# A two-layer diffusion trunk on one core: the shift's product as rows of the weight slab, the eviction moved behind six chunks, Q's rotary chunks in another order, and K's second copies by DMA

## The chip, the core and the metric

The kernel runs on one core of one Trainium2 chip. Times are device microseconds of one execution. The change is judged by the median of such times, beside runs of the kernel before. Five engines work side by side and meet only at semaphores: PE (TensorE, matrix products), ACT (ScalarE), DVE (VectorE), POOL (GpSimd) and SP, which here only issues DMAs.

## What is computed

Two layers over 768 tokens (256 of context, CTX, and 512 latent, LAT) of width 1024. Layer 0 mixes by gated linear attention, layer 1 by windowed attention with 16 query heads on 2 key heads. Each has a SwiGLU FFN of 2816 behind it. The part that matters here is how every projection gets its input, and what layer 1 does with Q and K:

```python
for i in range(DEPTH):
    hx = rmsnorm(x, norm_mix[i]) * (1.0 + sc1) + sh1        # sc, sh: scale and shift from silu(c) @ w_ada
    hc = rmsnorm(ctx, norm_mix[i]) * (1.0 + csc1) + csh1
    ox, oc = gla_mixer(hx, hc, ...) if i % 2 == 0 else swa_mixer(hx, hc, ..., cos, sin, not last)
    x = x + g1 * ox
    x = x + g2 * swiglu(rmsnorm(x, norm_ffn[i]) * (1.0 + sc2) + sh2, ffn_w_in[i], ffn_w_out[i])
    # the same for ctx, unless it is the last layer
# swa_mixer
q, k, v = jnp.split(h @ w_qkv + b_qkv, [SWA_Q, SWA_Q + SWA_KV], axis=-1)
qx = apply_rope(qx, cos, sin)
kx = apply_rope(kx, cos, sin)
# softmax over |i-j| <= 128, all context keys and a sink logit per head, then @ v and @ w_o
return rmsnorm(x, norm_final)
```

## The kernel before

**Slabs.** All weights come as slabs of 1024 rows by 256 columns (`w_raw`). Products are made in float32r: a slab is split into `w_hi` (ACT, function `split` of `act`, L1145) and `w_lo = w_raw - w_hi` (DVE, L1611), the input into a high and a low part as well, and PE makes three products, hi·hi, hi·lo and lo·hi. All of them have the line of the helper `mm`, L549. A slab has 8 chunks k of 128 rows. With both token segments a chunk is 12 matmuls (2 column blocks, 3 products, 256 and 512 columns), with LAT alone 6. Slab n lies in buffer n % 2. SP loads slab n+2 when PE has ended slab n.

**The slab without norm.** The first slab behind each residual sum starts before the norm is known: `first_slab` of `pe` multiplies `x * scale` (not normed), since `(x * rstd * scale + shift) @ w = rstd * ((x * scale) @ w) + shift @ w`. There are three: slab F0 (first slab of layer 0's FFN, both segments), KV0 (K and V of layer 1, both segments) and F1 (first slab of layer 1's FFN, LAT alone). In between its chunks PE also sums the squares (`statistics`, at k = 3) and spreads 1/rms over the partitions (`spread`, at k = 4, with LAT alone at k = 5), and ACT copies that into `rb` (`spread_out`, L1179). At the end PE makes `shift @ w`: for each of 2 column blocks and 8 chunks three matmuls with the weights as stationary operand and 2 moving columns (shift for LAT and for CTX, `sh_hi` and `sh_lo`), 48 in all.

**What DVE and ACT do meanwhile.** They make h, the normed input of the next slab, chunk by chunk: DVE `scaled` (L1666), ACT `h_hi` (L1190, `modulate`), DVE `h_lo` (L1675, `normal`). PE waits for each chunk of h in slab n+1. DVE's and ACT's queues are written out in order. After four chunks DVE waits for the end of slab n, copies `shift @ w` (`bz`, L1989 or L2089) and evicts the slab times `rb`; then chunks 4 to 7 follow. In the FFN ACT puts Silu on it. In slabs F0 and F0+1 PE also makes a piece of `silu(c) @ w_ada` (`unit`: 8 products with 32 stationary columns in four column groups of the array), which ACT copies to a row (`u_row`), PE turns with the 2-column matrix `sel`, and DVE adds to `mods`.

**K and Q of layer 1.** DVE evicts K into `y_rot`, ACT adds the bias, SP swaps the rotary halves by 4 DMAs of 32 partitions (`swap_halves`, L475), DVE makes cos and sin (L2068, L2072, L2077). ACT and DVE then write K's high and low part into `k_st`, each twice: heads 0 and 1, each into partitions 0 to 63 and 64 to 127 (L1488, L2108, 4 instructions each). Q has four slabs Q0 to Q0+3 and eight chunks f of 128 rows. For each, ACT `raw_q` (L1504) evicts and adds the bias, SP swaps, DVE turns (`turn_q`), ACT makes the high part (`high`, L1511) and DVE the low part (`low`, L2118). Slabs Q0+1 to Q0+3 are loaded into `ada_w`, one after the other: SP issues the next when DVE has ended `w_lo` of the one before. Behind it all come 64 rounds of attention: PE `scores`, DVE `maxima` (L2170), ACT exp (L1571), and so on, two rounds of scores ahead.

```python
        def raw_q(f):                       # act; may overwrite q_rot of f-3 only when low(f-3) is done
            if f < 7:
                act.wait_ge(ql_ok, max(2 * f - 3, 1))
```

Of the kernel before, what the change touches and what calls it, by code (L numbers as in the profile page):

```python
# [24 lines left out]
F32 = mybir.dt.float32  # L25
# [42 lines left out]
def trunk(nc, x, c, ctx_in, c_ctx, w_ada, b_ada, norm_mix, norm_ffn, gla_w_in, gla_w_gate_up, gla_b_gate_up,  # L68
# [159 lines left out]
    zg_ok, zp_ok, zk_ok = sems("zg_ok", "zp_ok", "zk_ok")  # L228
    amul_ok, t_ok, hh_ok, h_ok = sem("amul_ok"), sem("t_ok"), sem("hh_ok"), sem("h_ok")
# [16 lines left out]
    wp_ok = sem("wp_ok")  # L246
# [92 lines left out]
    def _(sp):  # L339
# [207 lines left out]
    def _(pe):  # L547
# [182 lines left out]
        def first_slab(n, e, segs, turn=None):  # L730
# [8 lines left out]
            for k in range(DC):  # L739
# [355 lines left out]

        pe.wait_ge(sink_ok, 9)
# [43 lines left out]
    def _(act):  # L1140
# [253 lines left out]
        def ffn(l, n0, segs):  # L1394
# [211 lines left out]
    def _(dve):  # L1606
# [369 lines left out]
        def ffn(l, m, n0, segs):  # L1976
# [3 lines left out]
            def first(n, sh):  # L1980
# [16 lines left out]
                normal(2 * l + 1, 2 * l, segs, sh, 4, 8)  # L1997
# [100 lines left out]
        normal(2, KV_EDGE, (LAT,), 48, 4, 8)  # L2098
# [170 lines left out]
```

## Time and profile before

| | us |
|---|---|
| median of 3 runs | 1707.42 |
| lowest and highest | 1706.73, 1715.22 |
| the profiled execution | 1717.53 |
| its span, first to last instruction | 1715.8 |
| PE busy | 1669.9 (97%) |
| DVE busy | 716.6 (42%) |
| ACT busy | 592.1 (35%) |
| TensorE's mean granted clock | 0.978 |

Busy time is the time in which an engine had an instruction under way. A busy PE can still be slow: the granted clock is 1.00 at 2.4 GHz and 0.50 at 1.2 GHz, and the page of the profile shows it per slice of the span. The rows further down are from four views: the timeline (instructions in order of time, merged where alike, with the idle time before one and what ended it), windows (busy time, granted clock and DMA share of a stretch), the DMA view, and the page itself.

### The profile page before, as it was taken

The page shows a single profiled execution, that of the slowest core. Times are in us where ns is not written, and L with a number is a line of the kernel's source. Part 1 is how long each engine was busy: PE and PEld are TensorE (multiplying, and loading weights), DVE is VectorE, ACT ScalarE, POOL GpSimd, SP SyncE. Part 2 cuts the span into 40 slices and gives each one's busy share as a digit, 9 for nine tenths or more (in the row PEclk, how much of TensorE's full clock was granted, in tenths as well). Part 3 has the DMA queues.
Part 4 walks back from the last instruction along what each step waited for, and adds up shares of the span by engine and source line. Part 5 has one row for each costly group of instructions (what it writes and reads, how often), then busy time and mean ns, then how long its engine had stood idle before and what let it go on. Part 6 is the DMA issues. An engine that isn't in the chain of part 4 may idle for free.

```text
span 1715.8 us, 24363 instructions
## 1 busy us (share of the span) xinstructions
PE 1669.9 (97%) x9948; PEld 1395.5 (81%) x9948; DVE 716.6 (42%) x1044; ACT 592.1 (35%) x890; POOL 103.4 (6%) x95
## 2 busy tenths in 40 slices
PE   7999999999999999999999999979999999999998
PEld 5889988888888888888888889756768888888886
DVE  5414536444532222222222245777764533333334
ACT  5224457443422211222111233457653422222223
POOL 0000000000000000000000000035550000000003
PEclk8999999999899999999999999979999899999999
DMA  9332200014243343343343322320002233333332
GB/s 337 88 123 92 81 25 26 25 58 139 74 124 98 108 137 98 113 132 98 119 127 98 92 68 74 86 68 2 2 1 74 74 98 98 98 98 98 89 90 91
DMA packets 197022, 155.30 MB, mean 91 GB/s; under 512 B 6658, under 2 KB 194222, under 8 KB 196942
## 3 DMA queue, kind: packets, MB, share of 16 engines
q1 hardware_dynamic: 196942, 154.18, 29.9%
q8 instruction: 57, 0.93, 0.2%
q14 instruction: 23, 0.19, 0.0%
HBM read 149.71 MB, written 2.10 MB: 88 GB/s over the span
## 4 chain that ended last, share of the span: by engine, by line
PE 89%; ACT 3%; DVE 3%; DMA 2%; SPq 1%; issue 1%; DVEq 0%; ACTq 0%
PE ps L549 87%; PE ps L1073 2%; DMA ada_pre<-in_w_ada 1%; ACT w_hi L1145 1%; DVE w_lo L1611 1%; DMA q_sw<-q_rot 0%; SPq L356 0%; DMA w_raw<-in_ffn_w_in 0%; DVE q_st L2118 0%; SPq L475 0%; PE ps L846 0%; DVE k_st L2108 0%; DVE r_act L1906 0%; ACT tmp L1285 0%; ACT k_st L1488 0%
## 5 line engine op out<-in xcount | busy, mean ns | idle before, releaser
L549 PE MATMUL ps<-h_hi,w_hi 128*128 128x256 f32 (+1 forms) x1392 | 422.2, 362 | 2.0 <-DVE w_lo L1611 1.5
L549 PE MATMUL ps<-h_lo,w_hi 128*128 128x256 f32 (+1 forms) x1392 | 411.1, 354 | 0.0
L549 PE MATMUL ps<-h_hi,w_lo 128*128 128x256 f32 (+1 forms) x1392 | 410.9, 354 | 0.0
L1611 DVE TENSOR_TENSOR w_lo<-w_raw,w_hi 128x2048 fp32r<-128x2048 f32 (+1 forms) x88 | 197.4, 2244 | 375.9 <-ACT w_hi L1145 375.8
L1145 ACT ACTIVATE w_hi<-w_raw 128x2048 fp32r<-128x2048 f32 (+1 forms) x88 | 165.1, 1876 | 408.9 <-DMA w_raw<-in_ffn_w_in 244.2
L549 PEld LDWEIGHTS ps<-h_hi,w_hi 128*128 128x128 f32 x1392 | 256.9, 190 | 49.6 <-issue 15.6
L549 PEld LDWEIGHTS ps<-h_lo,w_hi 128*128 128x128 f32 x1392 | 264.1, 190 | 36.9
L549 PEld LDWEIGHTS ps<-h_hi,w_lo 128*128 128x128 f32 x1392 | 263.9, 190 | 37.1
L549 PE MATMUL ps<-a_hi,w_hi 128*128 128x512 f32 (+1 forms) x528 | 159.7, 357 | 0.0
L549 PE MATMUL ps<-a_lo,w_hi 128*128 128x512 f32 (+1 forms) x528 | 157.9, 353 | 0.0
L549 PE MATMUL ps<-a_hi,w_lo 128*128 128x512 f32 (+1 forms) x528 | 157.8, 353 | 0.0
L537 POOL TENSOR_SCALAR pr<-pr,rden 128x384 f32<-128x384 f32 x64 | 84.1, 1314 | 896.2 <-DVE rden L2203 896.1
L549 PEld LDWEIGHTS ps<-a_hi,w_hi 128*128 128x128 f32 x528 | 98.0, 188 | 17.5 <-issue 4.1
L549 PEld LDWEIGHTS ps<-a_hi,w_lo 128*128 128x128 f32 x528 | 99.2, 188 | 14.2
L549 PEld LDWEIGHTS ps<-a_lo,w_hi 128*128 128x128 f32 x528 | 99.2, 188 | 14.0
L1426 ACT ACTIVATE tmp<-ps 128x512 f32<-128x512 f32 (+1 forms) x63 | 30.8, 524 | 199.4 <-PE ps L549 199.4
L1693 DVE SCALAR_TENSOR_TENSOR xT<-ps,mods,xT 128x256 f32<-128x256 f32 (+3 forms) x96 | 57.7, 657 | 98.5 <-PE ps L549 98.5
L2019 DVE TENSOR_TENSOR tmp<-tmp,ps 128x512 f32<-128x512 f32 (+1 forms) x63 | 35.8, 596 | 138.2 <-ACT tmp L1426 138.2
L549 PEld LDWEIGHTS ps<-k_st,q_st 128*128 128x128 f32 x320 | 44.2, 198 | 32.8 <-issue 21.1
L549 PE MATMUL ps<-k_st,q_st 128*128 128x256 f32 x320 | 55.3, 305 | 10.5 <-ACT pr L1571 10.5
L2170 DVE TENSOR_REDUCE row_max<-ps 128x1 f32<-128x513 f32 (+1 forms) x64 | 48.4, 756 | 27.6 <-PE ps L549 27.4
L1159 ACT ACTIVATE sq<-xT 128x768 f32<-128x768 f32 (+1 forms) x32 | 23.7, 740 | 101.0 <-DVE xT L1693 100.8
(242 smaller groups left out, 2043.4 us busy)
## 6 DMA issues: line engine op xcount, KB each, us to landing
w_raw<-in_ffn_w_in SPq DMA_DIRECT2D x88, 512.0 KB, 5.2
ada_w<-in_w_ada SPq DMA_DIRECT2D x41, 1024.0 KB, 5.4
w_raw<-in_ffn_w_out SPq DMA_DIRECT2D x32, 512.0 KB, 5.6
w_raw<-in_gla_w_in SPq DMA_DIRECT2D x24, 512.0 KB, 5.0
ada_pre<-in_w_ada SPq DMA_DIRECT2D x7, 1024.0 KB, 11.3
w_raw<-in_ffn_w_out SPq DMA_DIRECT2D x16, 384.0 KB, 3.7
w_raw<-in_gla_w_o SPq DMA_DIRECT2D x8, 512.0 KB, 7.1
w_raw<-in_swa_w_o SPq DMA_DIRECT2D x8, 512.0 KB, 4.6
```

What stands on the lines that cost most here:

```text
L537: pool.tensor_scalar(pr[i % 3][:, 0:384], pr[i % 3][:, 0:384], rden[:, i % 4:i % 4 + 1], None, ALU.mult)\
L549: return pe.matmul(o, w, r, start=start, stop=stop, skip_group_check=skip)
L1073: last = pe.transpose(bank(bk, (t - a) * P, P), pr[i % 3][:, t * P:(t + 1) * P], ident[:, :])
L1145: act.activation(w_hi[s][:, 0:kc, :], raw_of(n)[:, 0:kc, :], ACT.Copy).then_inc(whi_ok, 1)
L1159: act.activation(sq[ch % 2][:, a:T], xT[:, ch, a:T], ACT.Square).then_inc(sq_ok, 1)
L1426: last = act.activation(tmp[s][:, sg[0]:sg[1]], seg(3 * s, 0, sg), ACT.Silu)
L1611: dve.tensor_tensor(w_lo[s][:, 0:kc, :], raw_of(n)[:, 0:kc, :], w_hi[s][:, 0:kc, :].bitcast(F32), ALU.subtract).then_inc(wlo_ok, 1)
L1693: last = dve.scalar_tensor_tensor(xs, seg(3 * s, ch, sg), mods[:, bass.ds(gate + d0 + ch, 1), int(sg == CTX)], xs, ALU.mult, ALU.add)
L2019: last = dve.tensor_tensor(tmp[2 + s][:, sg[0]:sg[1]], tmp[s][:, sg[0]:sg[1]], seg(3 * s, 1, sg), ALU.mult)
L2170: dve.tensor_reduce(row_max[:, i % 4:i % 4 + 1], ps[:, b0 * 512:b0 * 512 + nk + 1], AX.X, ALU.max)\
```

## The change

There are four parts.

1. `shift @ w` is made with the shift as stationary operand: `sh_c` holds per chunk 32 columns, two of them the shifts and the rest zero, and the moving operand is the weight chunk of 256 columns in plain float32, `w_hi` and then `w_lo`. The 16 products go to four column groups of the array, 32 PSUM partitions each. They stand ahead of chunk k = 6 in the slab. ACT copies the result to `b_row` (`bias_row`), and at the slab's end PE turns it with `sel`, two products of 2 columns, which also sum the four groups.
2. In the three stages ACT copies `rb` before it splits the next slab. DVE makes chunk 0 of h before it splits, and the eviction stands behind six chunks of h in F0 and F1 (before: four), behind all eight in KV0.
3. `raw_q(7)` stands behind `high(6)`; `high` and `low` of f = 2 stand behind `turn_q(3)` on DVE; `low(6)` moves behind the first reciprocal of the attention rounds.
4. ACT and DVE write each half of K once. The other copy of each head is a DMA from `k_st` to `k_st`, 64 partitions each, issued by SP behind the swap of f = 1 and ahead of the load of slab Q0+3. PE waits for both ahead of the first scores.

```diff
@@ tiles
-    sh_hi = at("sh_hi", TM + 10 * ROW, [P, DC, 2], F32R)
-    sh_lo = at("sh_lo", TM + 10 * ROW + 64, [P, DC, 2], F32R)
+    sh_c = at("sh_c", TM + 10 * ROW, [P, DC, 32])
+    b_row = at("b_row", TM + 4 * ROW, [P, 256])
@@ sync
             swap_halves(f + 2, q_rot[sw_set(f)], q_sw[sw_set(f)], sw_in[sw_set(f)])
+            if f == 1:
+                sp.wait_ge(ql_ok, 1)
+                for g in range(2):
+                    sp.dma_start(k_st[64 - 64 * g:128 - 64 * g, :, g, :].bitcast(F32),
+                                 k_st[64 * g:64 * g + 64, :, g, :].bitcast(F32))\
+                      .then_inc(in_k, 16)
@@ tensor, first_slab
+                if k == 6:
+                    pe.wait_ge(rbs_ok, e + 1)
+                    pe.wait_ge(sh_ok, 2 * e + 2)
+                    for j, w in enumerate((w_hi, w_lo)):
+                        for c_ in range(DC):
+                            g = 32 * (c_ % 4)
+                            last = mm(bank(7, 0, 256)[g:g + 32, :], sh_c[:, c_, :], w[s][:, c_, :].bitcast(F32),
+                                      j == 0 and c_ < 4, j == 1 and c_ >= 4)
+                    last.then_inc(bw_done, 1)
...
-            pe.wait_ge(rbs_ok, e + 1)
-            pe.wait_ge(sh_ok, 2 * e + 2)
+            pe.wait_ge(br_ok, e + 1)
             for ch in range(2):
-                blk = slice(ch * P, (ch + 1) * P)
-                for k in range(DC):
-                    for j, (w, r) in enumerate(((w_hi, sh_hi), (w_hi, sh_lo), (w_lo, sh_hi))):
-                        last = mm(bank(7, 2 * ch, 2), w[s][:, k, blk], r[:, k, :], k == 0 and j == 0,
-                                  k == DC - 1 and j == 2, skip=True)
+                last = mm(bank(7, 2 * ch, 2), b_row[:, ch * P:(ch + 1) * P], sel[:, :], True, True)
             last.then_inc(slab_done, 1)
@@ scalar
+        def bias_row(e):
+            act.wait_ge(bw_done, e + 1)
+            act.activation(b_row[:, :], bank(7, 0, 256), ACT.Copy).then_inc(br_ok, 1)
@@ scalar, F0 and F1
+                spread_out(5 + 2 * l, a)
                 split(n + 1)
-                spread_out(5 + 2 * l, a)
-                modulate(2 * l + 1, 2 * l, segs, sh, 0, 4)
+                modulate(2 * l + 1, 2 * l, segs, sh, 0, 2)
+                bias_row(2 * l)
+                modulate(2 * l + 1, 2 * l, segs, sh, 2, 6)
...
-                modulate(2 * l + 1, 2 * l, segs, sh, 4, 6)
+                modulate(2 * l + 1, 2 * l, segs, sh, 6, 8)
                 split(n + 2)
-                modulate(2 * l + 1, 2 * l, segs, sh, 6, 8)
@@ scalar, KV0 and Q
+        spread_out(6, 0)
         split(Q0)
-        spread_out(6, 0)
-        modulate(2, KV_EDGE, (LAT,), 48, 0, 4)
+        modulate(2, KV_EDGE, (LAT,), 48, 0, 2)
+        bias_row(KV_EDGE)
+        modulate(2, KV_EDGE, (LAT,), 48, 2, 8)
...
-        modulate(2, KV_EDGE, (LAT,), 48, 4, 6)
         split(Q0 + 1)
-        modulate(2, KV_EDGE, (LAT,), 48, 6, 8)
         act.wait_ge(yr_ok, 1)
         for g in range(2):
-            for r in range(2):
-                last = act.activation(k_st[64 * r:64 * r + 64, 0, g, :], y_rot[64 * g:64 * g + 64, :], ACT.Copy)
+            last = act.activation(k_st[64 * g:64 * g + 64, 0, g, :], y_rot[64 * g:64 * g + 64, :], ACT.Copy)
...
-        for f in range(4, DC):
-            raw_q(f)
-            high(f - 1)
+        raw_q(4)
+        high(3)
+        raw_q(5)
+        high(4)
+        raw_q(6)
+        high(5)
+        high(6)
+        raw_q(7)
@@ vector, F0 and F1 (KV0: 0 to 1, split, 1 to 8, then the eviction)
+                normal(2 * l + 1, 2 * l, segs, sh, 0, 1)
                 split(n + 1)
-                normal(2 * l + 1, 2 * l, segs, sh, 0, 4)
+                normal(2 * l + 1, 2 * l, segs, sh, 1, 6)
                 dve.wait_ge(slab_done, n + 1)
...
-                normal(2 * l + 1, 2 * l, segs, sh, 4, 8)
+                normal(2 * l + 1, 2 * l, segs, sh, 6, 8)
                 split(n + 2)
@@ vector, K's low part: two instructions of four; Q and the first attention round
+        turn_q(3)
         low(2)
-        turn_q(3)
...
         turn_q(6)
-        low(6)
...
+            if i == 0:
+                low(6)
```

Three places show what stands in the queues. First PE, at the end of slab F0 (`w_hi_56` and `w_lo_60` are its weights, `w_hi_57` those of slab F0+1); chunk 5's last products, before and after:

```order
L549 MATMUL ps<-h_hi,w_lo_60 128x512
L549 MATMUL ps<-sh_hi,w_hi_56 128x2
L549 MATMUL ps<-sh_lo,w_hi_56 128x2
L549 MATMUL ps<-sh_hi,w_lo_60 128x2
...
L549 MATMUL ps<-ada_w,c_pre 32x256 x8
L549 MATMUL ps<-h_hi,w_hi_57 128x256
```

```order
L557 MATMUL ps<-h_lo,w_hi_56 128x512
L557 MATMUL ps<-h_hi,w_lo_60 128x256
L557 MATMUL ps<-h_hi,w_lo_60 128x512
L557 MATMUL ps<-w_hi_56,sh_c 32x256 x8
L557 MATMUL ps<-w_lo_60,sh_c 32x256 x8
L557 MATMUL ps<-h_hi,w_hi_56 128x256
L557 MATMUL ps<-h_hi,w_hi_56 128x512
```

Of before this is the slab's end (the three kinds with `sh` stand there 16 times each); of after it is the border of chunks 5 and 6, with two chunks of the slab still behind it.

Second DVE in stage F1, from 1/rms on (`w_lo_60` belongs to slab F1+1, `tmp` is the evicted slab):

```order
L1631 RECIPROCAL rstd<-std 128x4
L1611 TENSOR_TENSOR w_lo_60<-w_raw_58,w_hi_56 128x2048
L1666 SCALAR_TENSOR_TENSOR scaled_126<-xT,amul,rb 128x512
L1666 SCALAR_TENSOR_TENSOR scaled_127<-xT,amul,rb 128x512
L1675 SCALAR_TENSOR_TENSOR h_lo<-scaled_126,mods,h_hi 128x512
```

```order
L1655 RECIPROCAL rstd<-std 128x4
L1689 SCALAR_TENSOR_TENSOR scaled_126<-xT,amul,rb 128x512
L1698 SCALAR_TENSOR_TENSOR h_lo<-scaled_126,mods,h_hi 128x512
L1635 TENSOR_TENSOR w_lo_60<-w_raw_58,w_hi_56 128x2048
L1689 SCALAR_TENSOR_TENSOR scaled_127<-xT,amul,rb 128x512
L1689 SCALAR_TENSOR_TENSOR scaled_126<-xT,amul,rb 128x512
L1698 SCALAR_TENSOR_TENSOR h_lo<-scaled_127,mods,h_hi 128x512
```

The scaling of chunk 1 moved from ahead of the first `h_lo` to behind `w_lo`. It is what ACT's chunk 1 of h waits for, and `bias_row` stands behind that.

Third DVE in Q, from the turning of f = 2 (`q_rot_110`) on:

```order
L2077 TENSOR_TENSOR q_rot_110<-q_rot_110,q_sw_114 128x512
L1611 TENSOR_TENSOR w_lo_60<-ada_w,w_hi_56 128x2048
L2118 TENSOR_TENSOR q_st<-q_rot_110,q_st 64x512 x2
L2068 TENSOR_TENSOR q_rot_108<-q_rot_108,cosT 128x512
L2072 TENSOR_TENSOR q_sw_112<-q_sw_112,sinT 128x512
L2077 TENSOR_TENSOR q_rot_108<-q_rot_108,q_sw_112 128x512
L2118 TENSOR_TENSOR q_st<-q_rot_108,q_st 64x512 x2
```

```order
L2101 TENSOR_TENSOR q_rot_110<-q_rot_110,q_sw_114 128x512
L1635 TENSOR_TENSOR w_lo_60<-ada_w,w_hi_56 128x2048
L2092 TENSOR_TENSOR q_rot_108<-q_rot_108,cosT 128x512
L2096 TENSOR_TENSOR q_sw_112<-q_sw_112,sinT 128x512
L2101 TENSOR_TENSOR q_rot_108<-q_rot_108,q_sw_112 128x512
L2141 TENSOR_TENSOR q_st<-q_rot_110,q_st 64x512 x2
L2141 TENSOR_TENSOR q_st<-q_rot_108,q_st 64x512 x2
```

The low part of f = 2 now stands behind the turning of f = 3; the other pairs of turning and low part stay as they were, except that of f = 6.

## Rows read from the trace of the kernel before

**Rows 1.** Timeline of PE, stage F0: start, us, instruction, count.
```profile
457.72 0.51 PE L549 MATMUL ps<-h_hi,w_lo 128*128 128x256 f32 x2
458.07 0.16 PE L549 MATMUL ps<-sh_hi,w_hi 128*128 128x2 f32 x1
...
465.39 1.93 PE L549 MATMUL ps<-ada_w,c_pre 128*32 128x256 f32 x16
...
481.93 0.50 PE L549 MATMUL ps<-sel,u_row 128*128 128x2 f32 x4
...
486.70 1.07 PE L549 MATMUL ps<-ada_w,c_pre 128*32 128x256 f32 x16
487.70 0.62 PE L549 MATMUL ps<-h_hi,w_hi 128*128 128x256 f32 x2
```

**Rows 2.** Windows of F0: us, busy PE, PEld, DVE, ACT, POOL, PEclk, DMA, GB/s.
```profile
455.00:461.00 6.00, 6.00 (x47) 5.63 (x45) 5.29 (x10) 2.96 (x5) 0.00 (x0) 1.00 0.01 3
461.00:471.00 10.00, 10.00 (x51) 8.23 (x51) 4.29 (x10) 3.92 (x7) 0.00 (x0) 0.51 0.23 70
```

**Rows 3.** Timeline of DVE, stage F0.
```profile
449.17 2.29 DVE L1611 TENSOR_TENSOR w_lo<-w_raw,w_hi 128x2048 fp32r<-128x2048 f32 x1 [2.28 <-ACT w_hi L1145]
...
455.05 0.48 DVE L1666 SCALAR_TENSOR_TENSOR scaled<-xT,amul,rb 128x256 f32<-128x256 f32 x1
...
457.25 0.48 DVE L1666 SCALAR_TENSOR_TENSOR scaled<-xT,amul,rb 128x256 f32<-128x256 f32 x1
...
466.51 1.01 DVE L1994 TENSOR_TENSOR tmp<-ps,rb 128x256 f32<-128x256 f32 x2
```

**Rows 4.** Timeline of ACT, stage F0.
```profile
449.93 0.81 ACT L1179 ACTIVATE rb<-ps 128x768 f32<-128x768 f32 x1 [0.79 <-PE ps L549]
...
477.01 1.92 ACT L1145 ACTIVATE w_hi<-w_raw 128x2048 fp32r<-128x2048 f32 x1 [4.26 <-DMA w_raw<-in_ffn_w_in]
```

**Rows 5.** Timeline of stage F1, all engines.
```profile
1339.07 0.60 ACT L1179 ACTIVATE rb<-ps 128x512 f32<-128x512 f32 x1 [0.89 <-PE ps L549]
...
1340.26 0.39 PE L549 MATMUL ps<-rs_hi,w_hi 128*128 128x512 f32 x1
...
1342.74 0.75 DVE L1666 SCALAR_TENSOR_TENSOR scaled<-xT,amul,rb 128x512 f32<-128x512 f32 x1
...
1344.19 0.75 DVE L1666 SCALAR_TENSOR_TENSOR scaled<-xT,amul,rb 128x512 f32<-128x512 f32 x1
...
1364.11 0.39 PE L549 MATMUL ps<-h_hi,w_hi 128*128 128x512 f32 x1
```

**Rows 6.** Timeline of K, Q and the first attention round, all engines.
```profile
1076.11 1.12 ACT L1475 ACTIVATE y_rot<-y_rot,bz 128x256 f32<-128x256 f32 x2 [11.38 <-DVE y_rot L2093]
...
1083.40 2.29 DVE L1611 TENSOR_TENSOR w_lo<-ada_w,w_hi 128x2048 fp32r<-128x2048 f32 x1
...
1087.65 3.42 ACT L1488 ACTIVATE k_st<-y_rot 64x768 fp32r<-64x768 f32 x4 [4.95 <-DVE y_rot L2077]
...
1091.10 3.85 DVE L2108 TENSOR_TENSOR k_st<-y_rot,k_st 64x768 fp32r<-64x768 f32 x4 [3.48 <-ACT k_st L1488]
...
1107.85 0.69 DVE L2068 TENSOR_TENSOR q_rot<-q_rot,cosT 128x512 f32<-128x512 f32 x1 [0.68 <-DMA q_sw<-q_rot]
...
1129.88 1.40 DVE L2118 TENSOR_TENSOR q_st<-q_rot,q_st 64x512 fp32r<-64x512 f32 x2 [0.69 <-ACT q_st L1511]
...
1132.15 1.28 ACT L1571 ACT_TABLE_LOAD   x1 [1.65 <-DVE neg_max L2173]
...
1134.28 1.23 PE L549 MATMUL ps<-k_st,q_st 128*128 128x256 f32 x4 [9.48 <-ACT pr L1571]
```

**Rows 7.** DMA view, issues of 1060 to 1140: count, KB each, us to landing.
```profile
q_sw<-q_rot SPq DMA_DIRECT2D x32, 64.0 KB, 2.0
```

**Rows 8.** Windows in Q: slab load and swaps; swaps alone.
```profile
1104.00:1105.00 1.00, 1.00 (x6) 0.81 (x5) 0.97 (x2) 0.64 (x2) 0.00 (x0) 1.00 1.10 389
1113.00:1114.00 1.00, 1.00 (x6) 0.84 (x5) 0.97 (x2) 0.00 (x0) 0.00 (x0) 1.00 0.51 125
```

More of the change, by code:

```diff
@@ L155, in trunk @@
     rb = at("rb", TM + 9 * ROW, [P, T])
-    sh_hi = at("sh_hi", TM + 10 * ROW, [P, DC, 2], F32R)
-    sh_lo = at("sh_lo", TM + 10 * ROW + 64, [P, DC, 2], F32R)
-    bz = at("bz", TM + 10 * ROW + 128, [P, 2, 2])
+    sh_c = at("sh_c", TM + 10 * ROW, [P, DC, 32])
+    bz = at("bz", TM + 10 * ROW + 2048, [P, 2, 2])
+    b_row = at("b_row", TM + 4 * ROW, [P, 256])
     rs_hi = at("rs_hi", A, [P, DC, LX], F32R)
@@ L228, in trunk @@
     zg_ok, zp_ok, zk_ok = sems("zg_ok", "zp_ok", "zk_ok")
+    bw_done, br_ok, bt_done = sems("bw_done", "br_ok", "bt_done")
     amul_ok, t_ok, hh_ok, h_ok = sem("amul_ok"), sem("t_ok"), sem("hh_ok"), sem("h_ok")
@@ L244, in trunk @@
     osq_ok, f1_ok, f2_ok, goh_ok, go_ok = sems("osq_ok", "f1_ok", "f2_ok", "goh_ok", "go_ok")
-    wp_ok = sem("wp_ok")
+    wp_ok, in_k = sem("wp_ok"), sem("in_k")
     sw_in = sems("sw_in0", "sw_in1", "sw_in2", "sw_in3")
@@ L1093, in weighted @@
                 last.then_inc(pv_done, 1)
+        pe.wait_ge(in_k, 32)
         pe.wait_ge(sink_ok, 9)
@@ L1648, in shifts @@
         def shifts(e, sh):
-            dve.tensor_copy(sh_hi[:, :, :], mods[:, sh:sh + 8, :]).then_inc(sh_ok, 1)
+            dve.memset(sh_c[:, :, :], 0.0).then_inc(sh_ok, 1)
             dve.wait_ge(sh_ok, 2 * e + 1)
-            dve.tensor_tensor(sh_lo[:, :, :], mods[:, sh:sh + 8, :], sh_hi[:, :, :].bitcast(F32), ALU.subtract)\
-               .then_inc(sh_ok, 1)
+            dve.tensor_copy(sh_c[:, :, 0:2], mods[:, sh:sh + 8, :]).then_inc(sh_ok, 1)
         def normal(l, e, segs, sh, c0, c1):
@@ L2085, in _ @@
         inverse(6)
+        normal(2, KV_EDGE, (LAT,), 48, 0, 1)
         split(Q0)
-        normal(2, KV_EDGE, (LAT,), 48, 0, 4)
+        normal(2, KV_EDGE, (LAT,), 48, 1, 8)
         dve.wait_ge(slab_done, KV0 + 1)
@@ L2097, in _ @@
         dve.sem_inc(out_free[KV0 % 2], 1)
-        normal(2, KV_EDGE, (LAT,), 48, 4, 8)
         split(Q0 + 1)
@@ L2106, in _ @@
         for g in range(2):
-            for r in range(2):
-                last = dve.tensor_tensor(k_st[64 * r:64 * r + 64, 1, g, :], y_rot[64 * g:64 * g + 64, :],
-                                         k_st[64 * g:64 * g + 64, 0, g, :].bitcast(F32), ALU.subtract)
+            last = dve.tensor_tensor(k_st[64 * g:64 * g + 64, 1, g, :], y_rot[64 * g:64 * g + 64, :],
+                                     k_st[64 * g:64 * g + 64, 0, g, :].bitcast(F32), ALU.subtract)
         last.then_inc(ql_ok, 1)
```

## The prediction, made before the changed kernel ran

> **What bounds the kernel now.** I read the page first: PE is busy for nearly the whole span, so time can only come out of PE's own work, out of its clock, or out of the few stretches where it waits. Then the timeline of PE around the three slabs without norm, with the granted clock of the same stretches, and last DVE, ACT and SP there, since they say whether PE can use an earlier start.
>
> In stage F0 the 48 products of two columns run from 458.07 to the unit at 465.39: 7.3 us [rows 1]. The clock was 1.00 until 461 and 0.51 on the mean from 461 to 471, while PE worked without a gap [rows 2]: the products' first 3 us ran at 2.4 GHz, then all went at 1.2 GHz for 10 us. So the unit took 1.93 us where its like takes 1.07 at 486.70 [rows 1], and half of 5.6 us of ordinary work is lost behind the products. KV0 and F1 look alike.
>
> Between KV0 and attention PE does not set the pace: it stood for 9.48 us before 1134.28, until ACT had made the first exp. ACT's table load at 1132.15 waited for DVE's first maximum, and DVE came to it only with the last low part of Q, at 1129.88 [rows 6]. There the chain of DVE, ACT and SP is what counts, from K's first row at 1076.11 on.
>
> The sum is made against the profiled execution, 1717.53 us. The median of the runs is 10.1 us lower; I take the gain over to it unchanged, as all its terms lie on the chain that ends last in both.
>
> **Stage F0.** PE: slab F0's own products end at 458.07. A unit of 8 products costs 1.00 us from start to start at full clock (486.70 to 487.70), 16 cost 2.0, now inside the slab. So the slab ends at 460.1. The turning with sel is what stands at 481.93: 0.50 us, about 0.36 net, 460.5 [rows 1]. The unit follows, 461.5. ACT's b_row must be there at 460.1: rb is done at 450.74 [rows 4]; ACT splits until 452.6, makes chunk 0 until 453.7; DVE's h_lo until 454.45, its w_lo (2.25) until 456.7 [rows 3], scaled(1) until 457.8; ACT's chunk 1 until 458.5, b_row until 458.9. 1.2 us to spare.
>
> Slab F0+1 needs 8 chunks of 12 matmuls, pairs of them 0.347 us apart (457.72 to 458.07) [rows 1]: 16.7 plus a turning, from 461.5 to 478.5, if h keeps up. DVE makes a chunk in 2.20 us (455.05 to 457.25) [rows 3]: chunk 1 at 459.3, chunk 5 at 468.0, needed at 471.9. The eviction (1.9, as at 466.51 [rows 3]) and the table load for Silu (1.28, as at 1132.15 [rows 6]) push chunk 6 to 473.9 and chunk 7 to 476.1; PE comes to them at 474.4 and 476.4. It just fits. Late next is DVE: ACT splits slab F0+2 only behind chunk 7, 475.3 to 477.2, though its weights should have come by 471 (the wait for them ended at 477.01 [rows 4], and all goes 5.8 us earlier). DVE's w_lo ends at 479.5, the store to mods behind it at 479.7, and PE's next unit waits for that store: 1.2 us. Unit, then slab F0+2 at 480.75 instead of 487.70 [rows 1]: **7.0 us**. Bounds: 8.2 without that wait; 2 if the wait lowers the clock (up to half of 10 us, rows 2).
>
> **Stage F1.** There is no unit and a chunk is only 6 matmuls, 1.37 us. Chunk 6 starts at 1340.26 [rows 5]; plus 2.0 and two chunks the slab's products end at 1345.0. But b_row is late. rb is there at 1339.67 [rows 5]; ACT's split 1.9, chunk 0 0.7, DVE's h_lo 0.7, w_lo 2.25, scaled(1) 0.7, ACT's chunk 1 0.7, b_row 0.35: 1347.0. PE stands for 2.0 us, ends the slab at 1347.4 (before: 1351.0), and takes slab F1+1. DVE needs 1.45 us for a chunk (1342.74 to 1344.19) [rows 5]; chunk 5 is ready at 1352.5, then come the eviction and the Silu, chunk 6 at 1356.6, where PE wants it at 1355.6. Behind chunk 7 come ACT's split, until 1358.4, and w_lo, until 1360.65. Slab F1+2 starts at 1360.7 instead of 1364.11 [rows 5]: **3.4 us**, not the 7.6 that the removed products promise. Bounds: 2 (each of the 13 steps 0.1 later), 5 (PE alone).
>
> **KV0 to the first exp.** PE's slab ends 5 to 6 us earlier, as in F0, but DVE is not there. Before, ACT had done four chunks of h when its wait of 11.38 us began, at 1064.7 [rows 6], DVE at 1065.5. Now w_lo (2.25) and ACT's split (1.9) stand behind rb and no longer in the wait for it: 1069.7 for four chunks, and with four more at 1.45, less 0.5 at the end, 1075.0. Eviction and bias come behind them, so y_rot starts where it did, at 1076.2 (1076.11 [rows 6]), and the swap lands as before. What was queued between goes: ACT's split is done at 1080.1, DVE's w_lo starts at 1080.15 instead of 1083.40, 3.25 us. PE waits 1.6 us for it ahead of slab Q0+1; that is hidden. K's high part is 1.71 instead of 3.42, its low part 1.93 instead of 3.85 [rows 6]: 3.6 us. So raw_q(0) starts 6.9 us earlier, and so does w_lo of Q0+2.
>
> Then SP. The two copies of K carry 2 x 393 KB ahead of slab Q0+3 and the swap of f = 2, which DVE awaited at 1107.85 already [rows 6]. Swaps move 125 GB/s at a DMA share of 0.51 [rows 8], so 245 at full share: the copies take 3.2 us of it. Their two issues take 1.2 and lie before the slab's; with that the swap lands 2.3 us later against the rest: at about 1103.4, not 1107.85 minus 6.9. From here 4.45 us are left. Behind it the order saves: low(6), 1.40 us [rows 6], goes into the gap while PE makes the third scores, and turn_q(3) ahead of low(2) hides a wait for ACT of 0.7; with the waits for swaps as they now fall I get the table load at 1125.0 instead of 1132.15: **7.2 us**. Bounds: 10 if the copies cost nothing; 5 if they take twice their share. Raw_q(7) and its swap come late, at 1129.4; DVE wants it at 1129.5. PE's slab Q0+3 waits 3 us for w_lo; hidden, its end at 1118.7 is far ahead of the first maximum at 1123.
>
> The memset of sh_c and the copy take about 0.2 us more than the two casts they replace and end ahead of 1/rms; nothing.
>
> Sum: 7.0 + 7.2 + 3.4 = 17.6. 1717.5 - 17.6 = 1699.9; on the median 1707.4 - 17.6 = **1689.8 us**.
>
> The Trainium skill, "TensorEngine Tiling (Array Packing)", Key Properties, says that changing the tiling mode drains the array, and the block now stands inside a slab, with two changes more. By the trace the pair behind a unit takes 0.62 us (487.70) where 0.51 is usual (457.72) [rows 1]: 0.1 a change, so 0.6 us at most over three stages, which would make it 1690.4.
>
> The Trainium skill, "DMA: Bandwidth & Descriptors", Where 436 GB/s comes from, has SBUF to SBUF bound only by the fabric, at 435 GB/s. K's copies would be 1.8 us by it, an estimate, not 3.2. The rows show 125 GB/s in pieces of 2 KB; by the page the sum would be about 1.4 us better.
>
> **Rivals.**
> *The copies are cheap.* For it: a slab load moves 389 GB/s in rows 8, and K's pieces are 3 KB long. At that rate they take 2.0 us and the swap lands 1.2 earlier; at nothing 2.9. Time 1687 to 1689, taken as 1687.5. The page's rule on the fabric points here.
> *The new waits lower the clock.* PE now stands 1.2 us behind F0+1, 2.0 and 1.0 in F1. Against: they are short, the one before 1134.28 was 9.48 [rows 6]. For: nothing in the rows excludes it, and a stretch at half speed like that of rows 2 costs up to 5 us. In F0 it is fully exposed, in F1 partly: 5 to 8 us less gain, 1696.
> *The half speed was not the two-column products' alone.* The sums of squares, the spreading, the new block with 32 of 128 columns stationary, and sel now lie within 17 us. If the clock still falls, each of F0 and F1 gives back up to 5 us: 1699.8. Against: the clock was 1.00 from 455 to 461, behind the slab's statistics and spreading [rows 2], and the unit at 486.70 ran at full speed [rows 1].
> *Slower: the copies block SP's queue.* One swap DMA of 64 KB lands 2.0 us after issue [rows 7]. If a copy's time goes with its bytes at that pace, 393 KB take 12.3 us each, 24.6 together, 21.8 more than in my sum. Slab Q0+3, the swap of f = 2 and with them the whole chain of Q come later, and PE's first scores wait: 17.6 - 21.8 = -4.2, 1711.6. It decides from about 20 us for both copies. Against: several swap DMAs overlap, 0.6 us apart, at 125 GB/s, so 2.0 us is mostly latency.
>
> **How the numbers follow.** Forecast 0.62, copies cheap 0.13, waits lower the clock 0.13, half speed stays 0.08, slower 0.04. The forecast's own bounds are 1685 to 1695; with the cases beside it I take 1683 to 1700. What a measurement can tell from no change is 0.5%, 8.5 us. The forecast, the cheap copies and most of the third case gain more, 0.88; half speed stays and the rest of the third case are within, 0.08; slower 0.04.
>
> **What would show it.** PE's block of 32 matmuls of 256 columns takes 2.0 us, with the clock at 1.00 through all of F0 up to 480. b_row ends ahead of the slab in F0 and KV0, and PE waits about 2 us for it in F1. DVE's w_lo sets the start of slabs F0+2 and F1+2. The DMA k_st<-k_st takes 3 to 4 us and the wait for q_sw of f = 2 grows to about 3 us. The first exp is 13 to 15 us earlier, F0's gain counted in. I am wrong if the clock falls around 460, if PE waits for h in F0+1 by more than 1 us, or if the first exp comes late by a swap.

## The result and the profile after

| | before | changed |
|---|---|---|
| median, 12 runs each | 1712.82 us | 1700.05 us |
| lowest, highest | 1706.01, 1718.25 | 1696.43, 1701.98 |
| the profiled execution | 1717.53 | 1699.94 |
| its span | 1715.8 | 1698.2 |

The ratio is 0.9926, 95% interval 0.9907 to 0.9945: 12.8 us faster. I had 1689.8, range 1683 to 1700. Between the two profiled executions the gain is 17.6 us, as forecast; between the medians it is 4.8 us less, and before's median is 5.4 us above the one of three runs that I had started from (they are the first three of these twelve). Those two make the miss of 10.2 us. The 4.8 lies with before: its profiled execution was 4.7 us above its median, that of the changed kernel 0.1 below (1699.94 against 1700.05).

**F0.** Timeline of PE after, in the columns of [rows 1]:

```profile
453.33 1.07 PE L557 MATMUL ps<-w_hi,sh_c 128*32 128x256 f32 x16
454.21 1.05 PE L557 MATMUL ps<-w_lo,sh_c 128*32 128x256 f32 x16
...
459.53 0.50 PE L557 MATMUL ps<-sel,b_row 128*128 128x2 f32 x4
459.96 1.07 PE L557 MATMUL ps<-ada_w,c_pre 128*32 128x256 f32 x16
...
478.71 1.07 PE L557 MATMUL ps<-ada_w,c_pre 128*32 128x256 f32 x16 [0.39 <-DVE mods L1706]
```

PE's products with the shift (`sh_c`) now stand inside the slab; behind its last product come the turning (`sel`) and the unit, which takes 1.07 where it took 1.93. The wait for DVE's store to `mods` has come, 0.39 us in place of the 1.2 that I gave it. Windows of F0, KV0 and F1 after, in the columns of [rows 2]:

```profile
455.00:475.00 20.00, 20.00 (x134) 17.09 (x127) 17.99 (x34) 11.82 (x20) 0.00 (x0) 1.00 0.37 106
1062.00:1082.00 20.00, 18.38 (x85) 15.04 (x84) 13.88 (x19) 9.60 (x14) 0.00 (x0) 1.00 0.24 66
1334.00:1358.00 24.00, 21.95 (x96) 17.49 (x96) 15.76 (x20) 10.88 (x12) 0.00 (x0) 1.00 0.31 88
```

The granted clock is 1.00 in each: all three stages run at 2.4 GHz.

**K and Q.** Timeline of ACT, DVE and PE after, answering [rows 6]:

```profile
1068.25 1.12 ACT L1497 ACTIVATE y_rot<-y_rot,bz 128x256 f32<-128x256 f32 x2 [1.88 <-DVE y_rot L2118]
1072.23 2.29 DVE L1635 TENSOR_TENSOR w_lo<-ada_w,w_hi 128x2048 fp32r<-128x2048 f32 x1 [3.15 <-ACT w_hi L1159]
1076.49 1.70 ACT L1507 ACTIVATE k_st<-y_rot 64x768 fp32r<-64x768 f32 x2 [4.29 <-DVE y_rot L2101]
1078.22 1.92 DVE L2131 TENSOR_TENSOR k_st<-y_rot,k_st 64x768 fp32r<-64x768 f32 x2 [1.77 <-ACT k_st L1507]
...
1097.31 0.69 DVE L2092 TENSOR_TENSOR q_rot<-q_rot,cosT 128x512 f32<-128x512 f32 x1 [4.95 <-DMA q_sw<-q_rot]
...
1118.91 1.28 ACT L1595 ACT_TABLE_LOAD   x1
...
1121.04 0.93 PE L557 MATMUL ps<-k_st,q_st 128*128 128x256 f32 x4 [3.89 <-ACT pr L1595]
```

K's halves cost half. But DVE waited 4.95 us for the swap of f = 2, where it had waited 0.68. PE in turn waited 4.75 us for `w_lo` of slab Q0+3, where I had 3, and from there on ran at half speed:

```profile
1101.63 0.76 PE L557 MATMUL ps<-h_hi,w_hi 128*128 128x512 f32 x1 [4.75 <-DVE w_lo L1635]
```

The granted clock was 0.50 from 1101 to 1107. It cost nothing here, but by little: PE's first scores started at 1115.49, and DVE came to the first maximum at 1116.78, straight from turning f = 6.

**F1.** Timeline after, all engines, answering [rows 5]:

```profile
1325.30 0.60 ACT L1193 ACTIVATE rb<-ps 128x512 f32<-128x512 f32 x1 [3.51 <-PE ps L557]
1325.79 1.91 ACT L1159 ACTIVATE w_hi<-w_raw 128x2048 fp32r<-128x2048 f32 x1
...
1329.01 2.28 DVE L1635 TENSOR_TENSOR w_lo<-w_raw,w_hi 128x2048 fp32r<-128x2048 f32 x1
...
1332.62 0.36 ACT L1198 ACTIVATE b_row<-ps 128x256 f32<-128x256 f32 x1
...
1333.03 0.61 PE L557 MATMUL ps<-sel,b_row 128*128 128x2 f32 x4 [1.56 <-ACT b_row L1198]
...
1342.94 0.50 PE L557 MATMUL ps<-h_hi,w_hi 128*128 128x512 f32 x1 [1.01 <-DVE h_lo L1698]
1346.98 0.49 PE L557 MATMUL ps<-h_hi,w_hi 128*128 128x512 f32 x1 [1.03 <-DVE w_lo L1635]
```

PE waits three times, for `b_row`, for chunk 6 and for `w_lo`. New too are ACT's 3.51 us of idling ahead of `rb`: its split now stands behind.

### The profile page after: what moved, and what is told of

The parts are those of the page before. It is cut to its first block, busy times and chain, and to the rows that moved or that the text cites. A ratio compares the mean times of both kernels' runs of the same rounds, so it can differ in the third digit from the quotient of the medians.

```text
span 1698.2 us, 24292 instructions
## 1 busy us (share of the span) xinstructions
PE 1649.9 (97%) x9912; PEld 1372.2 (81%) x9912; DVE 715.0 (42%) x1042; ACT 591.1 (35%) x891; POOL 104.0 (6%) x95
## 4 chain that ended last, share of the span: by engine, by line
PE 86%; ACT 5%; DVE 5%; DMA 1%; SPq 1%; issue 1%; DVEq 0%; ACTq 0%
PE ps L557 84%; PE ps L1086 2%; ACT w_hi L1159 1%; DVE w_lo L1635 1%; DVE h_lo L1698 1%; DVE scaled L1689 1%; DMA ada_pre<-in_w_ada 1%; SPq L357 1%; ACT h_hi L1209 0%; DMA q_sw<-q_rot 0%; DMA w_raw<-in_ffn_w_in 0%; SPq L476 0%; PE ps L859 0%; DVE r_act L1929 0%; ACT tmp L1304 0%
## 5 line engine op out<-in xcount | busy, mean ns | idle before, releaser
L2043 DVE TENSOR_TENSOR tmp<-tmp,ps 128x512 f32<-128x512 f32 (+1 forms) x63 | 35.8, 596 | 140.1 <-ACT tmp L1446 140.1
```

The lines of the kernel that those rows point to most:

```text
L2043: last = dve.tensor_tensor(tmp[2 + s][:, sg[0]:sg[1]], tmp[s][:, sg[0]:sg[1]], seg(3 * s, 1, sg), ALU.mult)
```

## Where the time went, stage by stage

Each row is one profiled execution. F0: rb of F0 to rb of KV0. Q: rb of KV0 to ACT's table load ahead of the first exp. F1: std of F1 to the third `a_lo` behind it, that of the first slab inside the loop. The last column is the us at half speed behind the shift's products in F0, KV0 and F1. All rows but "before" and "changed" are experiments, told below.

| kernel | execution | F0 | Q | F1 | at half speed |
|---|---|---|---|---|---|
| before | 1717.5 | 608.5 | 73.7 | 42.2 | 10.2, 10.2, 10.2 |
| before_3 | 1711.3 | 606.8 | 71.1 | 42.2 | 6.8, 6.8, 10.2 |
| before_4 | 1705.4 | 604.9 | 71.5 | 40.6 | 3.4, 6.8, 6.8 |
| q_only | 1709.5 | 605.9 | 71.5 | 42.2 | 3.4, 6.8, 10.2 |
| changed | 1699.9 | 601.2 | 68.4 | 38.95 | 0, 0, 0 |
| after_again | 1700.1 | 601.3 | 68.5 | 38.95 | 0, 0, 0 |
| block_only | 1697.7 | 601.0 | 66.75 | 35.9 | 0, 0, 0 |
| k_engines | 1700.4 | 601.2 | 67.45 | 38.9 | 0, 0, 3.4 |
| k_late | 1691.8 | 601.2 | 64.0 | 38.95 | 0, 0, 0 |
| old_ffn | 1694.5 | 601.3 | 68.0 | 35.9 | 0, 0, 0 |
| split_first | 1694.4 | 600.6 | 67.9 | 35.7 | 0, 0, 0 |
| combo | 1688.2 | 601.4 | 61.2 | 35.85 | 0, 0, 0 |
| best | 1685.2 | 600.8 | 61.5 | 35.8 | 0, 0, 0 |

From profile to profile F0 gave 7.3 us (forecast 7.0), Q 5.3 (7.2), F1 3.2 to the loop (3.4). The three make 15.8. The remaining 1.8 came from outside them: 0.7 ahead of rb of F0, 0.5 between the table load and F1, 0.6 behind F1. My sum had nothing there, and it is scatter as far as I can tell: the second profile of the changed kernel lies 0.8 above, 1.8 below and 1.1 above the first in these. That the profiles came out at 17.6 was partly luck.

## The experiments

**The spread of before.** No edit; the kernel before against itself, then two single profiles.

> The kernel before, unchanged, against itself. So far its executions lie at two levels, 1706 to 1708 and 1714 to 1718 us; the profiled one was at 1717.5 with a mean clock of 0.978, while the changed kernel's lie between 1696.4 and 1702.0. Theory A (the levels are the clock's): the time of an execution falls with its mean granted clock, 1 us for each 0.001 or so, the executions at 1707 show about 0.985, those at 1716 about 0.978, and a profile at the lower level shows one or two of the stretches at half speed shorter or gone that the profile at 1717.5 has (362 to 369, 1127 to 1141, 1147 to 1154). Rival B: the clock is the same at both levels, and they differ by a wait, for instance a DMA that lands late. If A holds, the gain of 17.6 us between two profiles isn't the gain between medians, since before was profiled at its upper level.

Measured: median 1711.36 against 1710.48, ratio 1.0008 (0.999 to 1.0026), 1705.85 to 1718.01. Theory A holds as to the clock: over 64 executions of before on four chips (these 12 and those run beside this and the later experiments), from 1704.2 to 1719.0 us, the mean clock runs from 0.987 down to 0.977, and 0.001 of it goes with 1.4 us, where A had about 1 (correlation -0.97). What I had taken for two levels is a spread. This profile fell on 1717.98, again at the top, so where the half speed goes it could not tell.

> The kernel before, unchanged, one profile more. Its two profiles so far fell on its longest executions (1717.5 and 1718.0, 77 us at half speed), while its executions reach down to 1704. With Q's parts alone changed a profile at 1709.5 showed the stretch behind F0's products of two columns 3.4 us long instead of 10.2, the one in KV0 6.8 instead of 10.2. Theory A: the length of these stretches changes from execution to execution by 3.4 us at a time; a profile below 1710 us shows F0, KV0 or F1 with less than 10.2 us each, and rb of F0 to rb of KV0 takes 605.9 where F0 has 3.4 us at half speed and 608.4 where it has 10.2. Rival B: the three stretches are always 10.2 us long in this kernel and the others, at the start, at 362 and in attention, make the spread.

> The same once more, with the same expectations: under A a profile below 1710 us has a shorter stretch at half speed in F0, KV0 or F1; under B all three are 10.2 us long again and the start, 362 to 369 and attention make the difference.

Measured: 1711.32 and 1705.35. Windows over the same three stages, of before, before_3 and before_4 in turn:

```profile
455.00:475.00 20.00, 20.00 (x117) 17.30 (x116) 12.78 (x25) 7.87 (x13) 0.00 (x0) 0.74 0.34 99
1062.00:1082.00 20.00, 20.00 (x99) 18.01 (x98) 9.72 (x17) 7.26 (x11) 0.00 (x0) 0.74 0.06 14
1334.00:1358.00 24.00, 24.00 (x119) 21.23 (x118) 15.18 (x23) 10.78 (x13) 0.00 (x0) 0.79 0.23 62
```

```profile
455.00:475.00 20.00, 20.00 (x125) 17.34 (x125) 13.73 (x27) 8.11 (x13) 0.00 (x0) 0.83 0.31 95
1062.00:1082.00 20.00, 20.00 (x105) 17.52 (x105) 11.74 (x18) 7.54 (x11) 0.00 (x0) 0.83 0.05 13
1334.00:1358.00 24.00, 24.00 (x111) 20.80 (x110) 16.20 (x23) 9.89 (x13) 0.00 (x0) 0.79 0.16 44
```

```profile
455.00:475.00 20.00, 20.00 (x133) 17.17 (x133) 11.68 (x24) 9.70 (x15) 0.00 (x0) 0.91 0.36 106
1062.00:1082.00 20.00, 20.00 (x92) 17.00 (x92) 11.95 (x17) 9.83 (x13) 0.00 (x0) 0.83 0.23 66
1334.00:1358.00 24.00, 24.00 (x110) 20.37 (x110) 13.72 (x19) 9.07 (x12) 0.00 (x0) 0.86 0.32 88
```

PE is busy throughout, and still the clock column of F0 reads 0.74, 0.83 or 0.91: (1 - 0.74) x 20 x 2 is 10.4 us at half speed, 0.83 gives 6.8, 0.91 gives 3.6. Theory A holds, B does not: the same products cost another amount in each execution. Only before_4 fell below 1710 us as A had asked; its F0 took 604.9 us where A had 605.9 for 3.4 us at half speed, and that one microsecond I did not follow. Against before_4 the changed kernel gains 3.7, 3.1 and 1.6 us in the three stages, 8.4; against the profile that I had, 7.3, 5.3 and 3.2, 15.8. In F0 the gain is 7.3, 5.6 and 3.7 where before had 10.2, 6.8 and 3.4 us at half speed; by that step some 2 us would be left without any (an estimate). The Trainium skill, "TensorE: Matmul & The Clock Gate", What's actually happening, says that the monitor's window runs free and does not restart with the kernel, so that a change of clock depends on where the work falls in it. The three profiles are in keeping with it, with 3.4, 6.8 and 10.2 us behind the same instructions in F0; that it is the reason no run here shows.

**The block alone.** Before with the shift's product as in the changed kernel, nothing else:

```diff
+                if k == 6:
+                    pe.wait_ge(rbs_ok, e + 1)
...
-                modulate(2 * l + 1, 2 * l, segs, sh, 0, 4)
+                modulate(2 * l + 1, 2 * l, segs, sh, 0, 2)
+                bias_row(2 * l)
+                modulate(2 * l + 1, 2 * l, segs, sh, 2, 4)
```

> The kernel before with the shift's product as 32 products of 256 columns inside the slab alone; the eviction stays behind four chunks of h, Q's order and K's copies as before. Theory A (the block is nearly all of the change): F0 gains 7 us, F1 2 to 4, and at KV0 the eviction starts 5.5 us earlier since DVE had waited for PE's slab there (four chunks were ready at 1065.5, the slab at 1074.9), and the whole chain of Q moves with it: 14.5 to 16.5 us off a profile at 1717.5, a median of 1698 to 1702. Rival B (as my sum had it, KV0's and Q's 7.2 us come out of the new order of ACT and DVE, the turning one ahead and K's copies): F0 and F1 gain 10.4 and KV0 to the first exp 1 to 2, a median near 1704. On the levels: if the 48 products of two columns make them, this kernel's executions lie within 6 us of each other as the changed kernel's; if not, two levels 10 us apart stay.

Measured: 1697.05 (1691.54 to 1697.77), ratio 0.9911 (0.9886 to 0.9936). Theory A, and beyond its numbers: its profile lies 19.8 us below 1717.5, where A had 14.5 to 16.5, and F1 gained 6.3, where A had 2 to 4. The block is all of the change, and F1 is 3 us shorter than in the changed kernel. The intervals of the two ratios overlap; the stage times set the two kernels apart. The granted clock was 1.00 in the windows of all three stages here as well. Timeline of ACT and DVE in its F1:

```profile
1322.62 1.92 ACT L1151 ACTIVATE w_hi<-w_raw 128x2048 fp32r<-128x2048 f32 x1 [0.74 <-DMA w_raw<-in_ffn_w_in]
1324.56 2.29 DVE L1626 TENSOR_TENSOR w_lo<-w_raw,w_hi 128x2048 fp32r<-128x2048 f32 x1 [2.48 <-ACT w_hi L1151]
1325.38 0.60 ACT L1185 ACTIVATE rb<-ps 128x512 f32<-128x512 f32 x1 [0.85 <-PE ps L550]
...
1328.84 0.36 ACT L1190 ACTIVATE b_row<-ps 128x256 f32<-128x256 f32 x1
```

Here split and w_lo lie in the time in which ACT and DVE wait for PE's spreading, and b_row is 3.9 us earlier, long before the slab ends. Its executions spread over 6.2 us, where I had 6 at most and before has 14.

**Q's parts alone.** Before, with K's copies by DMA and Q's order as in the changed kernel.

> The kernel before with Q's new order and K's second copies by DMA at their place in the changed kernel, the shift's product left as it was. Theory A: K's halves 3.6 and the order 2.1, less 4.3 of wait for the swap of f = 2, leave 1.4 us from rb of KV0 to the first exp, 73.3 against 74.7; median within 0.15% of before's. Rival B (the order and the copies bring what my sum had beside w_lo, 4 us): 70.7. On the levels: the executions spread over 10 to 14 us as before's do, since the stretches of two columns are still there, and the time goes with the clock; if its profile falls at a low level, it shows which stretches at half speed are missing there.

Measured: 1710.29 against 1709.32, ratio 1.0002 (0.9985 to 1.002). The median moved by less than 0.15% and the executions spread over 12.4 us, as A had it, and B's 4 us are out. From y_rot to the table load it took 55.1 us, against 56.0 in the profile of before, 55.5 in before_3 and 55.9 in before_4: 0.4 to 0.9 us, less than A's 1.4. The whole stage, 71.5 us, is no shorter than that of before_3 and before_4 (71.1 and 71.5), which had the same 6.8 us at half speed in KV0. The copies' wait takes back most of what K's halves save, as in the changed kernel.

**Where K's copies stand.** k_late is the changed kernel with one line other:

```diff
-            if f == 1:
+            if f == 3:
                 sp.wait_ge(ql_ok, 1)
```

k_engines has no DMA; both copies are ACT's and DVE's, four instructions each, as before.

> The changed kernel with K's two copies issued behind the swap of f = 3, no longer ahead of slab Q0+3's load and the swap of f = 2. DVE waited 4.95 us for that swap at 1097.31, where before it waited 0.68. Theory A (the copies' traffic and SP's queue delay the slab and the swap): that wait falls to about 0.7, ACT's wait for slab Q0+3 (4.54) to under 1, the first exp comes 3.5 to 4.5 us earlier, and the time falls to about 1696, in no case does PE wait for the copies ahead of the first scores. Rival B (the wait is the swaps' own, since the chain ahead of them is shorter by K's halves): the wait stays above 3 us and the time within 1 us of the changed kernel's 1700.

> The changed kernel with K's second copies made by ACT and DVE again (four instructions each in place of two, no DMA). Theory A (the DMA copies give back what they save): k_st's high and low parts cost 3.42 and 3.85 again, 3.6 us more on the chain, and the wait for the swap of f = 2 falls from 4.95 to 0.7 to 1.5; the time is within 1 us of the changed kernel's 1700. Rival B (the sum as forecast, copies worth 3.6 less 2.3): 1.3 us slower, 1701.4. Rival C (the copies are free and the wait is the swap's own): 3.6 us slower, 1703.6.

Measured: k_late 1695.46 (1691.38 to 1699.27), ratio 0.9917; k_engines 1699.77, 0.9931. DVE's wait for the swap of f = 2, in k_late and in k_engines:

```profile
1090.53 0.69 DVE L2092 TENSOR_TENSOR q_rot<-q_rot,cosT 128x512 f32<-128x512 f32 x1 [0.72 <-DMA q_sw<-q_rot]
```

```profile
1097.34 0.69 DVE L2085 TENSOR_TENSOR q_rot<-q_rot,cosT 128x512 f32<-128x512 f32 x1 [0.50 <-DMA q_sw<-q_rot]
```

Theory A for both, by the stage times; the ratios' intervals (0.9892 to 0.9942 and 0.9906 to 0.9957) overlap with that of the changed kernel. Behind the swap of f = 3 the copies make nothing wait and Q is 4.4 us shorter; ahead of slab Q0+3 they cost 4.2 us of waiting and save 3.6, and without them Q is 1.0 shorter. DMA view of the changed kernel, 1080 to 1110, in the columns of [rows 7], and its SP:

```profile
ada_w<-in_swa_w_qkv SPq DMA_DIRECT2D x2, 512.0 KB, 7.1
k_st<-k_st SPq DMA_DIRECT2D x2, 384.0 KB, 4.5
```

```profile
1085.94 1.36 SPq L487 DMA_DIRECT2D k_st<-k_st  x2
1087.35 3.01 SPq L357 DMA_DIRECT2D ada_w<-in_swa_w_qkv  x2
1090.40 5.01 SPq L476 DMA_DIRECT2D q_sw<-q_rot  x8
```

The two issues (1.36 us) hold back the slab's, and the slab's own two issues take 3.01 us. In k_late, where the copies come later, they take 1.16:

```profile
1083.38 1.16 SPq L357 DMA_DIRECT2D ada_w<-in_swa_w_qkv  x2
```

The slab's halves land 7.1 us after issue, not 5.1 as in k_late. The swap stands behind both: counted from rb of KV0, SP comes to it 3.2 us later than in k_late, and from there to DVE's turning it is 6.9 us where k_late has 5.9. That makes the 4.2.

**The order in F0 and F1.** The changed kernel with another order in its first FFN slab. split_first moves ACT's and DVE's split only:

```diff
+                split(n + 1)
                 spread_out(5 + 2 * l, a)
-                split(n + 1)
...
-                normal(2 * l + 1, 2 * l, segs, sh, 0, 1)
                 split(n + 1)
-                normal(2 * l + 1, 2 * l, segs, sh, 1, 6)
+                normal(2 * l + 1, 2 * l, segs, sh, 0, 6)
```

old_ffn moves the eviction back behind four chunks as well, and with it ACT's split of slab n+2 ahead of chunks 6 and 7 of h.

> The changed kernel with ACT's and DVE's old order in the first slabs of F0 and F1 (the weights' split ahead of the first chunk, eviction behind four chunks), KV0 and Q as changed. Theory A (the new order makes b_row late in F1): b_row is there before the slab ends, PE's waits of 1.56, 1.01 and 1.03 us fall to one of 0.8, F1 is 2.3 to 3 us shorter and F0 the same within 0.4: 2.5 to 3 us faster than the changed kernel on the same chip. Rival B (the eviction behind six chunks pays in F0, where a chunk takes DVE 2.2 us): F0 longer by 1 to 3 us and nothing gained in the sum.

> The changed kernel with the split of slab n + 1 (ACT's w_hi, DVE's w_lo) ahead of rb and the first chunk in F0 and F1, as before; the eviction stays behind six chunks. With this and the eviction behind four, F1 was 3.0 us shorter (the loop behind it starts 35.9 us after std instead of 38.95). Theory A (the split is what costs: ahead of rb it lies in ACT's wait of 3.5 us and DVE's of 3.9, behind rb it is on the chain): F1 is 2.5 to 3.2 us shorter than in the changed kernel, F0 the same within 0.4. Rival B (the eviction's place makes it): 1 us or less of it.

Measured: old_ffn 1695.32 (1694.47 to 1697.26) where the changed kernel on the same chip has 1699.27; split_first 1694.75 (four runs), ratio 0.99 (0.9859 to 0.9941). A in both, though not quite within its numbers: F1 is 3.0 us shorter in old_ffn, and 3.3 in split_first, where A had at most 3.2 and F0 came out 0.6 shorter where A had 0.4. In split_first only the split moved, so its place is the cause, and PE's waits of F1 shrink to one of 0.84. old_ffn's median fell by 3.9 us, where A had 2.5 to 3; the stages show the 3.0 and 0.5 in Q. Six chunks against four are worth 0.7 in F0 and 0.3 in F1; in the two kernels of the next part it is 0.6 and nothing.

> The changed kernel unchanged, on the chip of the three others, to compare them with and for a second profile. By the clock theory its executions lie at 1695 to 1702, their time going with the mean granted clock (0.985 to 0.993), and a profile differs from the first only in the stretches at half speed; stage for stage the rest repeats within 0.3 us (rb of KV0 to the first exp 69.7, F1 from rb to the end 373).

Measured: 1699.27 (1697.13 to 1701.06), ratio 0.9936 (0.9913 to 0.9959), stages within 0.1 us of the first profile. Before's median on that chip was 1709.32, so the gain there is 10.1 us, not 12.8: the changed kernel repeats within 0.8 us, and before's median moves.

**Together.** combo is block_only with Q's order and K's copies at f = 3; best has the eviction behind six chunks as well.

> The block for the shift, with the eviction behind four chunks and ACT's and DVE's old order in F0, KV0 and F1 (as in the kernel with the block alone), plus Q's new order and K's second copies by DMA behind the swap of f = 3. Theory A: the four savings add, since each was seen at its own place: the first exp comes 5.5 us earlier than with the block alone (3.6 for K's halves, 1.4 for low(6), 0.7 for the turning ahead), that is 62.5 us after rb of KV0 against 68.0, and F0 and F1 stay as with the block alone; median 5 to 6 us below it, about 1691 to 1692 where before has 1710.5. Rival B (Q is then bound by the swaps or by PE's slabs): the wait for a swap grows above 2 us, or PE's slab Q0+3 ends the wait for the first scores, and 2 to 3 us are left, 1694.

> The block, the split ahead of rb, the eviction behind six chunks in F0 and F1, KV0 in its old order, Q's new order and K's second copies by DMA behind the swap of f = 3. Six chunks against four, with the split ahead of rb in both, were worth 0.7 us from rb of F0 to rb of KV0 (600.6 against 601.3) and 0.3 in F1 (35.67 against 35.94). Theory A (these add to the kernel with the eviction behind four): 600.6 in F0, 62.5 from rb of KV0 to the first exp, 1688.5 us where before has 1709, a ratio of 0.988. Rival B (with four chunks the time had the same median, and the difference is within the clock's scatter): the ratio lies between 0.987 and 0.989 as well; then stage times alone can tell them apart.

Measured: combo 1689.62 (1688.12 to 1690.34), ratio 0.9881 (0.9856 to 0.9906), 62.5 us to the first exp as expected, the median a little under A's 1691 to 1692. best 1687.74 (1685.17 to 1691.0), ratio 0.9865 (0.9835 to 0.9894). Both beat the changed kernel, combo by 9.7 us on the same chip, best by its ratio to before, 0.9865 where the changed kernel has 0.9926 and 0.9936; the ratios' intervals overlap, so whether best beats combo stays open, as rival B had it. From the profiles only F0's 0.6 speaks for it, and Q's 0.4 against.

## Why the prediction was wrong

**The step that failed** is "The median of the runs is 10.1 us lower; I take the gain over to it unchanged, as all its terms lie on the chain that ends last in both." The terms do lie on the chain, but the one that matters is not the same in both. The profiled execution was among the slowest of its kernel, with the longest stretches that any profile showed, 10.2 us in each of three stages. Most of what the change removes from such an execution is that half speed, so it removes less from fast ones: 8.4 us in the three stages against before_4, 15.8 against the profile. The 10.1 us between profile and median was the first sign, and I read it as an offset. A gain of some 12, the middle of 8.4 and 15.8, would have given 1695 on my median; 12.8 and 10.1 were measured on two chips. The rest, 5.4 us, is the median of three runs of a kernel that spreads over 14: two of the three lay near its lower end.

**K's copies** were the term of wrong size: 2.3 us against the swap, measured 4.2. The transfer's 3.2 us at the swaps' rate stood up well, but I let most of the issues of 1.2 us run beside it, and had nothing for longer issues of the slab. The runs show 1.36 us for the copies' issues, 1.85 more for the slab's, and a swap that lands 1.0 later: together 4.2, about issue and transfer in full. Why the slab's issues grew no run shows. So Q gave 5.3, not 7.2. The Trainium skill, "DMA: Bandwidth & Descriptors", Where 436 GB/s comes from, would have had 1.8 us for the transfer; in k_late a window with the copies (and from 1094.60 on the next swap) moved 238 GB/s at a DMA share of 0.99, by which 786 KB take 3.3 us, and that decides:

```profile
1094.00:1096.00 2.00, 1.46 (x7) 1.00 (x6) 1.97 (x4) 0.58 (x1) 0.00 (x0) 1.00 0.99 238
```

The rival of cheap copies is out, and so is the one of a blocked queue: they landed in 4.5 us, not 12.3.

**What held.** F0: 7.3 for 7.0, with a wait for the store shorter than I had it since PE came to the unit 0.5 later and DVE's store 0.3 earlier; b_row had 1.6 us to spare. F1: w_lo sets slab F1+2, 3.4 us; PE's waits 1.56 and 1.01 for 2.0 and 1.0. KV0: y_rot starts where it did, w_lo 3.2 us earlier for 3.25, raw_q(0) 6.8 for 6.9. The order behind the swap gave 2.7. The block costs PE 2.0 us with its changes of mode, so nothing came on top of the sum's 2.0 for them:

```profile
1326.26 0.40 PE L557 MATMUL ps<-rs_hi,w_lo 128*128 128x512 f32 x1
1326.58 1.07 PE L557 MATMUL ps<-w_hi,sh_c 128*32 128x256 f32 x16
...
1328.45 0.50 PE L557 MATMUL ps<-rs_hi,w_hi 128*128 128x512 f32 x1
```

2.19 from start to start where 0.23 is usual. The half speed in the three stages was the two-column products' own: with the block alone, and all else as before, it is gone from all three. So the third rival is out, though its 1699.8 is near the time that came. The second is out for the changed kernel, whose F0 and F1 ran at 1.00 in both profiles. In Q the clock did fall behind a new wait, the 4.75 us ahead of slab Q0+3, at no cost here. In k_engines, with the same edits in F1, that stage had 3.4 us at half speed and was as long as without (38.9); why, I did not follow.

**What I did not ask** is what each part gives without the others. I counted KV0's and Q's gain as the new order's; with the block alone Q is 66.75 us, 1.7 shorter than in the changed kernel. DVE had stood at KV0 for a slab that now ends 5 to 6 us earlier, and the old order used that at once (y_rot 12.0 us behind rb, 17.8 in the changed kernel). By these stage times the reordering and the early copies gave back 4.7 us in Q and F1.

## What to carry to other kernels

Where a change removes work that runs at a reduced clock, take the price from several profiles or from the clocks of all runs, not from one execution; a profile far from the median says that the price moves. Put an engine's big independent piece (a split) ahead of what it has to wait for, not behind, and look at its idle time there before moving anything: here the place alone was worth 3.3 us in F1. A large copy in a queue with small ones that another engine waits for belongs behind them: here the copies held up the swap by 4.2 us, for a transfer of 3.3 and issues of 1.4.

## What the runs showed of the chip

PE without a gap can still fall to 1.2 GHz: behind 48 matmuls of two moving columns it ran at half speed for 3.4, 6.8 or 10.2 us, changing between executions of one program, and with the block in their place it did not. And profiled executions need not lie in the middle of the runs: two of the four of before fell on 1717.5 and 1718.0 in a spread from 1704.2 to 1719.0.
